# Two of four modulation pieces on VectorE, and another order of the opening, in a fused two-block fp32 kernel

## The reference

```python
# first block, front
c_act = silu(c)
mod = c_act @ w_mod[l] + b_mod[l]              # 2048 x 12288 weights, one row of activations
sh1, sc1, g1, sh2, sc2, g2 = split(mod, 6)
h = rmsnorm(x, norm1_w[l]) * (1.0 + sc1) + sh1
proj = h @ w_in[l]                             # q, k, v, z, xbc, dt, gates
...
bias = bias_table[bucket]                      # added to the attention logits
...
# second block, side product
e = rms_norm(p[l] @ w_ple[l], ple_gain[l])
```

## Time and profile before

| | us |
|---|---|
| median of 3 executions | 3271.97 (3269.01 to 3273.8) |
| profiled execution, whole | 3274.9 |
| its span, first to last instruction | 3272.8 |
| TensorE busy in the span | 3204.1 |
| VectorE busy | 2274.3 |
| ScalarE busy | 1534.3 |
| mean granted TensorE clock | 0.997 |

### The profile page before, as it was taken

How to read it: one execution, slowest core, us unless ns; L and a number is a source line. 1 busy time by engine, 2 the same in 40 slices (tenths; PEclk the granted TensorE clock), 3 DMA queues, 4 the chain that set the end, 5 groups by cost and what they waited for, 6 DMA issues and landing times.

```text
span 3272.8 us, 52356 instructions
## 1 busy us (share of the span) xinstructions
PE 3204.1 (98%) x22201; PEld 2931.9 (90%) x22201; DVE 2274.3 (69%) x2774; ACT 1534.3 (47%) x1560; POOL 0.2 (0%) x4
## 2 busy tenths in 40 slices
PE   7999999999999999999999999999999999999999
PEld 5788989988998898988888888899899999999987
DVE  6697578887787788777776556776555655555676
ACT  3334656634554344433333333476655474433433
POOL 0000000000000000000000000000000000000000
PEclk9999999999999999999999999999999999999999
DMA  9996555566555676556665566544633444455554
GB/s 397 389 354 232 190 193 193 193 250 224 177 186 195 243 271 245 217 220 243 230 225 201 183 202 204 189 178 171 216 133 139 165 171 153 157 181 207 207 191 155
DMA packets 105805, 693.03 MB, mean 212 GB/s; under 512 B 11519, under 2 KB 18751, under 8 KB 30180
## 3 DMA queue, kind: packets, MB, share of 16 engines
q1 hardware_dynamic: 93168, 655.30, 54.9%
q10 hardware_dynamic: 12404, 34.38, 2.9%
HBM read 679.05 MB, written 13.72 MB: 212 GB/s over the span
## 4 chain that ended last, share of the span: by engine, by line
PE 86%; DVE 6%; DMA 2%; ACT 2%; DVEq 2%; issue 1%; ACTq 0%; SPq 0%
PE accp L511 27%; PE accp L512 14%; PE accp L516 11%; PE accp L517 11%; PE accp L518 11%; DVE wlo L1604 2%; DMA raw<-w 2%; PE accp L514 2%; ACT whi L1083 1%; DVE macc L1667 1%; DVEq L1669 1%; PE pw L1021 1%; PE pw L583 1%; PE pw L593 1%; PE pw L986 1%
## 5 line engine op out<-in xcount | busy, mean ns | idle before, releaser
L1604 DVE TENSOR_TENSOR wlo<-raw,whi 128x2048 fp32r<-128x2048 f32 (+1 forms) x544 | 1202.3, 2210 | 503.1 <-ACT whi L1083 497.4
L1083 ACT ACTIVATE whi<-raw 128x2048 fp32r<-128x2048 f32 (+1 forms) x544 | 1002.6, 1846 | 610.6 <-DMA raw<-w 582.9
L511 PE MATMUL accp<-act,whi 128*128 128x512 f32 x2550 | 910.6, 399 | 6.9 <-DVE qkv L1614 5.2
L516 PE MATMUL accp<-act,whi 128*128 128x256 f32 x2912 | 840.8, 289 | 9.4 <-DVE wlo L1604 4.3
L517 PE MATMUL accp<-act,whi 128*128 128x256 f32 x2912 | 824.7, 283 | 0.0
L518 PE MATMUL accp<-act,wlo 128*128 128x256 f32 x2912 | 824.6, 283 | 0.0
L512 PE MATMUL accp<-act,wlo 128*128 128x256 f32 x2720 | 735.5, 281 | 0.0
L511 PEld LDWEIGHTS accp<-act,whi 128*128 128x128 f32 x2550 | 479.6, 188 | 118.7 <-DVE qkv L1614 6.9
L516 PEld LDWEIGHTS accp<-act,whi 128*128 128x128 f32 x2912 | 559.2, 192 | 17.6 <-issue 7.1
L517 PEld LDWEIGHTS accp<-act,whi 128*128 128x128 f32 x2912 | 559.6, 192 | 5.3 <-issue 5.0
L518 PEld LDWEIGHTS accp<-act,wlo 128*128 128x128 f32 x2912 | 559.2, 192 | 0.0
(11 more groups left out here) (507 smaller groups left out, 4157.3 us busy)
## 6 DMA issues: line engine op xcount, KB each, us to landing
raw<-w SPq DMA_DIRECT2D x480, 1024.0 KB, 4.8
raw<-w SPq DMA_DIRECT2D x64, 704.0 KB, 4.1
mraw_a<-wm SPq DMA_DIRECT2D x42, 1024.0 KB, 11.3
mraw_b<-wm SPq DMA_DIRECT2D x16, 1024.0 KB, 8.2
mraw_c<-wm SPq DMA_DIRECT2D x16, 1024.0 KB, 6.9
mraw_x<-wm SPq DMA_DIRECT2D x10, 1024.0 KB, 13.4
acb<-ac_d ACTq DMA_DIRECT2D x8, 1024.0 KB, 4.7
mraw_w<-wm SPq DMA_DIRECT2D x8, 1024.0 KB, 7.5
```

Source lines behind the costliest of these rows:

```text
L511: pe.matmul(acc, wh, both, start=first, stop=False, skip_group_check=True)
L516: pe.matmul(acc[:, 0:S], wh, x2[:, 0, :], start=first, stop=False)
L1083: act.activation(whi[:, c % 4, 0:k, :], raw[:, c % 4, 0:k, :], ACT.Copy).then_inc(hi_done, 1)
L1604: dve.tensor_tensor(wlo[:, c % 4, 0:k, :], raw[:, c % 4, 0:k, :], whi[:, c % 4, 0:k, :].bitcast(F32), ALU.subtract).then_inc(lo_done, 1)
```

## The change

Five things are changed, all in the front.

1. VectorE makes pieces 0 and 1 of batches 1 to 7 (`mod_quarter` runs over j = 0, 1: eight operations and not four), TensorE pieces 2 and 3. Both counters and SP's waits for slots follow.
2. TensorE makes the rows of its two pieces in one group ahead of tile 9. Before, its three pieces stood ahead of tiles 4, 7 and 10.
3. In the opening on ScalarE, the rounding of chunk 0 comes ahead of the copies of the bias rows, and the third `embed_take` ahead of the square root.
4. In the opening on VectorE, `lo(1)` comes behind the first of four adds that sum the squares; on TensorE, `mod_rows(0, 0)` and the first half of the second `ple` chunk come ahead of `rms_summed`.
5. The five stores are issued inside the loop, at n = 6, and not behind it.

```diff
--- before.py
+++ after.py
@@ -436,14 +436,14 @@
 
                 for a, b, _, ring in MSTAGES:
                     if 32 <= m and 4 * a <= m < 4 * b:
-                        sp.wait_ge(mod_used_d, 7)
-                        sp.wait_ge(mod_used, max(32, 4 * a, m - ring + 1) - 7)
+                        sp.wait_ge(mod_used_d, 14)
+                        sp.wait_ge(mod_used, max(32, 4 * a, m - ring + 1) - 14)
                 if 6 <= m < 32:
                     before = m - 6
-                    if before >= 4 and before % 4 == 0:
-                        sp.wait_ge(mod_used_d, before // 4)
+                    if before >= 4 and before % 4 < 2:
+                        sp.wait_ge(mod_used_d, 2 * (before // 4) - 1 + before % 4)
                     else:
-                        sp.wait_ge(mod_used, before + 1 - before // 4)
+                        sp.wait_ge(mod_used, before + 1 - 2 * (before // 4))
                 b = MORDER[m // 4]
                 sp.dma_start(mod_slot(m), wm[one(b), m % 4].rearrange("a p k n -> p (a k) n")).then_inc(mod_landed(m)[0], 16)
 
@@ -585,7 +585,7 @@
 
             def mod_rows(n, j):
 
-                j0 = 1 if n else 0
+                j0 = 2 if n else 0
                 if j == j0 and n >= 2:
                     pe.wait_ge(mod_ok, n - 1)
                 pe.wait_ge(*mod_landed(4 * n + j))
@@ -624,11 +624,11 @@
             mm.then_inc(brow_mm, 1)
             pe.wait_ge(p_ok, 1)
             halves(C0["ple"], E0["ple"], lambda k: p2[:, k], 2, ms=2)
-            rms_summed(1, S, sqX[:, 0, :])
             embed = lambda h: halves(C0["ple"] + 1, E0["ple"] + 4, lambda k: p2[:, k], 2, ms=2, hs=(h,))
             mod_rows(0, 0)
+            embed(0)
+            rms_summed(1, S, sqX[:, 0, :])
             mod_rows(0, 1)
-            embed(0)
             mod_rows(0, 2)
             embed(1)
             mod_rows(0, 3)
@@ -636,8 +636,9 @@
             pe.wait_ge(brow_ev, 1)
             for n in range(8):
                 for i in range(24):
-                    if n < 7 and i in (4, 7, 10):
-                        mod_rows(n + 1, i // 3)
+                    if n < 7 and i == 9:
+                        for j in range(2, 4):
+                            mod_rows(n + 1, j)
                     if n < 7 and i == 13:
                         mod_block(n + 1)
                     if n == 0 and i == 8:
@@ -1122,13 +1123,13 @@
             for n in range(2):
                 act.activation(nudge[:, n:n + 1], C("c", n, 1), ACT.Copy).then_inc(silu_d, 1)
             act.activation(nudge[:, 2:3], C("c"), ACT.Copy).then_inc(s0_ev, 1)
+            hi(0)
             act.wait_ge(brow_mm, 1)
             for g in range(3):
                 ins = act.activation(brow[:, g, :], pw[0:4, 1 + g, :], ACT.Copy)
             ins.then_inc(brow_ev, 1)
             act.wait_ge(brow_ev, 1)
             act.dma_start(br_d, brow[:, :, :].rearrange("j g n -> j (g n)")).then_inc(brow_st, 16)
-            hi(0)
             act.wait_ge(x_in, 16)
             act.activation(sqX[:, 8:16, :], xT[:, 8:16, :], ACT.Square).then_inc(e_sq, 1)
 
@@ -1154,9 +1155,9 @@
             embed_take(0, 0)
             hi(1)
             embed_take(0, 1)
+            embed_take(1, 0)
             root(1, rstd[:, :], sqT[:, 0, :])
             hi(C0["qs"])
-            embed_take(1, 0)
             embed_take(1, 1)
             act.wait_ge(brow_st, 16)
             for n in range(8):
@@ -1167,11 +1168,12 @@
                 hi_eighth(n)
                 if n % 2 == 0:
                     hi(C0["qs"] + 3 * (n // 2) + 1)
+                if n == 6:
+                    act.wait_ge(*out_of(8))
+                    act.dma_start(e_d, e0T[:, :, :].rearrange("p k n -> p (k n)")).then_inc(e_st, 16)
+                    for j in range(4):
+                        act.dma_start(bw_d[j], br_d[j:j + 1, :].to_broadcast([P, 1536])).then_inc(brow_st, 16)
             hi(C0["qs"] + 11)
-            act.wait_ge(*out_of(8))
-            act.dma_start(e_d, e0T[:, :, :].rearrange("p k n -> p (k n)")).then_inc(e_st, 16)
-            for j in range(4):
-                act.dma_start(bw_d[j], br_d[j:j + 1, :].to_broadcast([P, 1536])).then_inc(brow_st, 16)
             hi(C0["qkv"])
             for g in range(3):
                 act.wait_ge(used, 2 * C0["qkv"] - 2 + g)
@@ -1759,18 +1761,23 @@
 
             def mod_quarter(n):
 
-                src = mod_slot(4 * n)
-                dve.wait_ge(*mod_landed(4 * n))
-                dve.tensor_scalar(macd[:, :], src[:, 0, :], cact[:, 0:1], None, ALU.mult)
-                for k in range(1, 4):
+                for j in range(2):
+                    src = mod_slot(4 * n + j)
+                    dve.wait_ge(*mod_landed(4 * n + j))
+                    for k in range(4):
+                        a = 4 * j + k
+                        if a == 0:
+                            ins = dve.tensor_scalar(macd[:, :], src[:, 0, :], cact[:, 0:1], None, ALU.mult)
+                        else:
+                            ins = dve.scalar_tensor_tensor(macd[:, :], src[:, k, :], cact[:, a:a + 1], macd[:, :], ALU.mult, ALU.add)
+                        if k < 3:
+                            dve.drain()
+                    ins.then_inc(mod_used_d, 1)
                     dve.drain()
-                    ins = dve.scalar_tensor_tensor(macd[:, :], src[:, k, :], cact[:, k:k + 1], macd[:, :], ALU.mult, ALU.add)
-                ins.then_inc(mod_used_d, 1)
-                dve.drain()
 
             def mod_join(n):
 
-                dve.wait_ge(mod_used, 3 * n + 4)
+                dve.wait_ge(mod_used, 2 * n + 4)
                 if n >= 2:
                     dve.wait_ge(mod_mm, n - 1)
                 dve.tensor_tensor(MACC[n][:, :], MBANK[n % 2], macd[:, :], ALU.add).then_inc(macc_ok, 1)
@@ -1784,8 +1791,9 @@
             for k in (8, 4, 2, 1):
                 dve.drain()
                 dve.tensor_tensor(sqX[:, 0:k, :], sqX[:, 0:k, :], sqX[:, k:2 * k, :], ALU.add)
+                if k == 8:
+                    lo(1)
             dve.drain().then_inc(rq, 1)
-            lo(1)
             rms_root(1, pw[:, 4, 0:S], sqT[:, 1, :], D, sems=((rm, 1), rv, (rs, 1), sqT[:, 2, :], sqT[:, 0, :]))
             normed(0)
             for n in range(8):
```

## The result

| | us |
|---|---|
| before, median of 9 executions | 3273.8 (3269.01 to 3275.22) |
| changed kernel, median of 9 | 3280.61 (3277.62 to 3285.51) |
| ratio | 1.0025, 95% interval 1.0016 to 1.0033 |
| span of the profiled execution | 3278.7 (before 3272.8) |

The change makes the kernel slower by 0.25%, or 5.2 to 10.8 us by the interval; between the medians it is 6.8 us. The time lies just inside the stated range, but on the other side of the bound for "no change".

The account below looks back on a forecast made before the run. TensorE, busy 3204.1 of 3272.8 us, was taken as the bound, so only its long part's start could move. Loop +13.3, opening -4.0 and rest -7.5 gave +1.8: 3273.8 us against the median 3271.97, range 3268 to 3281.5.

Parts of the forecast that it names:

- VectorE leads the even turns: Loop of the eighths: VectorE is the chain in even turns, four more operations add 3.3 us each; whole loop +13.3 us.
- The opening: Until batch 0 is finished, 38.69 us before: the earlier rounding and reordered rows save 4.0 us, bounds -7.8 and -1.
- The rest: From the eighth mod_finish to the twelfth qkv chunk: earlier stores let qkv loads land sooner, -7.5 us, bounds 0 and -9.
- a gap between the stores' end and the qkv loads: Behind the loop: stores through at about 142 us, first qkv loads at about 146, so they would not meet.
- TensorE's clock: Loop: new TensorE waits ahead of tile 13 may lower its clock, +1.7 us or +3.4; a rival, chance 0.12.
- rival C: The clock case: new waits in the loop lower TensorE's clock, 3275.5 us, or 3277.2 if odd turns tip over; chance 0.12.
- The sum: Whole front: loop +13.3, opening -4.0 and rest -7.5 give +1.8 us; this forecast had chance 0.60.
- The chance of 0.17 for "slower": Whole kernel: the probability given to a result slower by over 0.2% (6.5 us); within that bound 0.77, faster 0.06.

Follow-up runs that it names:

- e3: Changed kernel with extra matmuls, results dropped, on TensorE ahead of each mod_block of the loop, so that it stays busy: 3276.0 us, ratio to before 1.0011.
- e1: Kernel before with only the opening's edits on ScalarE, VectorE and TensorE: 3269.17 us, ratio to before 0.9992.
- e4: Changed kernel with the five stores put back behind the loop: 3284.96 us, ratio to before 1.0039.
- e7: Changed kernel with the five stores issued at about 229 us, behind the rounding of the fifteenth qkv chunk: 3287.04 us, ratio to before 1.0051.
- e5: Kernel before with only the five stores moved into the loop at n = 6, profiled twice: 3268.27 us, ratio to before 0.9994.
- f2: Kernel before with the new opening and TensorE's rows in one group ahead of tile 9, VectorE making one piece: 3267.82 us, ratio to before 0.9990.

## Why the prediction was wrong

**VectorE leads the even turns: right.** Four more operations of 0.83 us stretched them by 3.3 with the clock up (16.95 in e3), the odd ones by 0.5 (0.6 forecast), the last by 1.8 (1.6): 13.1 against 13.3.

**The opening: right**, -3.75 against -4.0, with the root, the squares and the rows in the order worked out (TensorE starts at 13.65, forecast 13.45; the copy of batch 0 comes at 33.20, forecast 33.0). A part of the exact match is luck: over all profiles the opening is worth 4.4.

**The rest: right in size** (-7.8 against -7.5), half wrong in its cause: 5.6 by the stores, 2.2 by the slower loop. It stood on a gap between the stores' end and the qkv loads. There was one, though not where it was forecast: the stores were issued at 130.6 and ran until about 154 us, not from 128 to 142, and it is the late end of the loop, 159.80, that kept the gap open. A part of what came back is the clock as well: before the change TensorE waits 4.8 us for VectorE in this stretch, behind the late load, and then runs slow, as the second of these two stretches shows. That is 4 x 0.40 = 1.6 us lost, which the forecast did not know of as such. So the close match in size is in part luck:

```profile
164.00:168.00 4.00, 1.40 (x7) 1.26 (x8) 2.91 (x5) 1.91 (x1) 0.00 (x0) 0.97 1.02 430
168.00:172.00 4.00, 4.00 (x15) 3.39 (x15) 3.85 (x4) 1.58 (x1) 0.00 (x0) 0.60 1.01 428
```

**TensorE's clock: the failed step.** It stood in the text as rival C with +1.7 us and a chance of 0.12, and I left it out of the sum, as if the new waits cost nothing there. It should have been a term, and it measured 5.6 us. The mechanism was named rightly, its price was half of what it is and one place was missing. The fall at 40 us that I read in the earlier trace rows costs 1.7 us; each of the four behind a wait of 3 to 5 us took nearly twice that. From the rows of 144 to 152 us: 4 x 0.50 + 4 x 0.28 = 3.1 us lost; read in stretches of 1 us, and only where TensorE is busy, the four lose 3.4, 3.2, 2.9 and 3.4. (Nor is 1.7 the rule for the short wait: in e1 the fall in the opening began while TensorE still stood idle, and by the rows below it lost 1.75 x 0.50 + 4 x 0.30 = 2.1.) And I had counted as hidden all that falls into a turn. But the mod_block for which VectorE waits runs right behind TensorE's wait, and so in the slow stretch; from join to finish it is more than the 1.83 us of before in all four such turns (2.33, 2.65, 2.64, 2.32), and one odd turn took 14.10. These five differences make 2.6 and 0.5 us, the 3.1 of the loop. Behind the last wait nothing hides it: 2.55 us. The Trainium skill (TensorE: Matmul & The Clock Gate, Why this matters for your kernels) warns of idle gaps between bursts of matmuls, and the trace bears it out with four falls to 1.2 GHz behind waits of 3.0 to 5.1 us. I cited it and then priced it from one short case.

The stretches of e1 in which its first eighth begins:

```profile
36.00:40.00 4.00, 1.75 (x8) 1.78 (x9) 2.18 (x4) 2.43 (x2) 0.00 (x0) 0.50 1.02 424
40.00:44.00 4.00, 4.00 (x27) 2.21 (x26) 3.83 (x5) 1.92 (x1) 0.00 (x0) 0.70 1.02 424
```

**The sum** came near to zero by three large terms of opposite signs, so that 5.6 us left out of it decided the outcome. The chance of 0.17 for "slower" was too low for that: the bounds of the three terms were each several us wide, and the sum can't be surer than they are.

## What to carry to other kernels

Work moved from one engine to another is judged turn by turn, not by busy shares: VectorE was 70% busy, and still had nothing to give in every second turn, where a piece cost 3.3 us; in the others it cost about 0.5, and gained nothing that a run here could show. A wait put in front of TensorE costs more than its length if the instruction behind it is the one that others wait for, since it then runs at the lower clock; short extra matmuls in the wait show at once how much that is. Big stores belong where the DMA engines have a gap that can be seen in the stretches, and that gap moves with the speed of the loop around it.

## What the runs showed of the hardware

Behind four waits of 3.0 to 5.1 us on TensorE the granted clock went to 1.2 GHz and cost 2.9 to 3.4 us each time. The length of the wait does not give the price: behind the 2.8 us wait in the opening it was 1.7 us before the change and 2.1 to 2.3 in e1, behind waits of 2.9 (before, at 167 us), 2.2 (e4) and 1.8 us (e7) it was 1.7, behind one of 2.6 in the second profile of e5's kernel 4.7, and behind one of 2.3 in f2 there was no fall. With matmuls in the loop's waits, of which no result was used, the clock stayed at 2.4 GHz from 42 us to the end of the loop (e3).

The loads of 1 MB behind the loop took 12.51, 15.20, 16.06 and 16.20 us with 5.24 MB of stores under way on the other queue, and each stands in the chain of waits. The rule that an engine takes turns between the queues that have work (the Trainium skill, DMA: Bandwidth & Descriptors, Queues, rings and completion order) fits that, but no run shows the turns themselves. Nor do the long loads alone show the stores' part. In the loops of e1 and f2, with none of the five stores issued yet, some loads took about as long:

```profile
58.68 11.50 DMA raw<-w
```

```profile
56.96 15.44 DMA mraw_a<-wm
```

What shows it is e7 against the changed kernel, where the place of the stores alone made 8.1 us. And two profiles of one kernel can differ by 4.7 us in the first 215 us: a term of the sum that is smaller than this needs medians, or the same stretch in several profiles.
